# Conditioning weights loaded directly behind the block of the input projection that they follow, instead of a block on

## What is computed

```python
mod_x = (silu_c @ w_mod[i] + b_mod[i])[:, None, :]
mod_c = silu_cc @ w_mod[i] + b_mod[i]
sh_x, sc_x, g_x = jnp.split(mod_x, 3, axis=-1)
hx = rms_norm(x, norm_g[i]) * (1.0 + sc_x) + sh_x
...
px = hx @ w_in
q = apply_axial_rope(rms_norm(q, q_g), cos, sin)
...
x = x + g_x * yx
```

## Time and profile before

| | us |
|---|---|
| median of 3 runs | 2017.3 |
| lowest, highest | 2016.65, 2020.82 |
| the profiled execution | 2018.24 |
| its span (first to last instruction) | 2016.4 |
| mean granted TensorE clock | 0.985 |

### The profile page before, as it was taken

How to read it: one execution, slowest core, us unless ns; L and a number is a source line. 1 busy time by engine, 2 the same in 40 slices (tenths; PEclk the granted TensorE clock), 3 DMA queues, 4 the chain that set the end, 5 groups by cost and what they waited for, 6 DMA issues and landing times.

```text
span 2016.4 us, 28017 instructions
## 1 busy us (share of the span) xinstructions
PE 1916.3 (95%) x10575; PEld 1579.1 (78%) x10575; DVE 1455.0 (72%) x1546; ACT 1194.3 (59%) x1289; POOL 73.3 (4%) x66
## 2 busy tenths in 40 slices
PE   6999998998899899999889999999999999999997
PEld 4776677885687799998668888888888888888886
DVE  3655835227667665566588898989889898898985
ACT  3335815236456543444467777777777777777774
POOL 0110000003000000000010000000000000000000
PEclk9999999999999999999979999999999999999999
DMA  8451035436437355553469999999999999999993
GB/s 324 140 196 62 2 137 186 136 94 87 117 124 209 105 188 188 187 193 126 163 232 376 384 355 382 363 363 382 354 382 350 372 370 356 387 354 383 361 368 114
DMA packets 277031, 501.60 MB, mean 249 GB/s; under 512 B 26232, under 2 KB 53280, under 8 KB 276944
## 3 DMA queue, kind: packets, MB, share of 16 engines
q1 hardware_dynamic: 273648, 491.82, 69.8%
q0 software_dynamic: 2240, 8.03, 1.1%
q10 hardware_dynamic: 1056, 0.57, 0.1%
HBM read 498.25 MB, written 2.12 MB: 248 GB/s over the span
## 4 chain that ended last, share of the span: by engine, by line
PE 74%; issue 11%; DVE 7%; ACT 4%; DMA 2%; SPq 1%; POOL 1%; ACTq 0%; DVEq 0%; POOLq 0%
PE bank L1896 21%; PE bank L1897 21%; PE bank L1898 21%; SPq L667 1%; DVE w_lo L1154 1%; PE bank L2075 1%; ACT w_hi L767 1%; PE bank L2089 1%; PE bank L2365 1%; PE bank L2064 1%; DMA raw<-in_w_mod 1%; PE bank L1918 1%; PE bank L2127 1%; PE bank L2156 1%; PE bank L2399 1%
## 5 line engine op out<-in xcount | busy, mean ns | idle before, releaser
L1662 DVE TENSOR_TENSOR w_lo<-raw,w_hi 128x2048 fp32r<-128x2048 f32 x168 | 381.1, 2288 | 50.8 <-ACT w_hi L1057 50.8
L1662 DVE TENSOR_TENSOR w_lo_x<-raw_x,w_hi_x 128x2048 fp32r<-128x2048 f32 x168 | 382.8, 2290 | 42.0 <-ACT w_hi_x L1057 40.9
L1057 ACT ACTIVATE w_hi_x<-raw_x 128x2048 fp32r<-128x2048 f32 x168 | 323.2, 1924 | 128.7 <-PE bank L1898 126.7
L1154 DVE TENSOR_TENSOR w_lo<-raw,w_hi 128x2048 fp32r<-128x2048 f32 x98 | 224.1, 2290 | 217.7 <-ACT w_hi L767 217.6
L1057 ACT ACTIVATE w_hi<-raw 128x2048 fp32r<-128x2048 f32 x168 | 322.2, 1919 | 47.3 <-PE bank L1898 46.8
L767 ACT ACTIVATE w_hi<-raw 128x2048 fp32r<-128x2048 f32 x98 | 186.9, 1909 | 174.3 <-PE bank L1898 126.6
L1896 PE MATMUL bank<-h_hi,w_hi 128*128 128x256 f32 (+1 forms) x864 | 260.7, 302 | 4.6 <-DVE w_lo L1154 3.1
L1897 PE MATMUL bank<-h_lo,w_hi 128*128 128x256 f32 (+1 forms) x864 | 258.1, 299 | 0.0
L1898 PE MATMUL bank<-h_hi,w_lo 128*128 128x256 f32 (+1 forms) x864 | 258.0, 299 | 0.0
L1896 PE MATMUL bank<-w_hi,xe_hi 128*128 128x512 f32 x612 | 244.2, 399 | 0.0
L1898 PE MATMUL bank<-w_hi,xe_lo 128*128 128x512 f32 x612 | 239.7, 392 | 0.0
(11 more groups left out here) (322 smaller groups left out, 3097.1 us busy)
## 6 DMA issues: line engine op xcount, KB each, us to landing
raw<-in_e_w SPq DMA_DIRECT2D x168, 1024.0 KB, 7.0
raw_x<-in_e_w SPq DMA_DIRECT2D x168, 1024.0 KB, 7.6
raw<-in_w SPq DMA_DIRECT2D x33, 1024.0 KB, 5.1
raw<-in_w_qkv SPq DMA_DIRECT2D x24, 1024.0 KB, 5.2
raw<-in_w_mod SPq DMA_DIRECT2D x19, 1024.0 KB, 5.3
raw<-in_b_w_in SPq DMA_DIRECT2D x16, 1024.0 KB, 5.8
raw<-in_a_w_in SPq DMA_DIRECT2D x9, 1024.0 KB, 7.3
raw<-in_w_o SPq DMA_DIRECT2D x8, 1024.0 KB, 5.5
```

The costliest lines, as they stand in the source:

```text
L1057: nc.scalar.activation(ring6(w_hi, w_hi_x, n, 1)[:, 0, :], ring6(raw, raw_x, n, 1)[:, 0, :], ACT.Copy).then_inc(x_hi_ready, 1)
L1154: nc.vector.tensor_tensor(w_lo[:, split_slot(m), :], raw_unit(m), w_hi[:, split_slot(m), :].bitcast(F32), ALU.subtract).then_inc(lo_ready, 1)
L1662: nc.vector.tensor_tensor(ring6(w_lo, w_lo_x, n, 1)[:, 0, :], ring6(raw, raw_x, n, 1)[:, 0, :], ring6(w_hi, w_hi_x, n, 1)[:, 0, :].bitcast ...
```

## The change

```diff
@@ -116,8 +116,8 @@
             if (name, cb) == ("a_in", 0):
                 mod_columns(*mods_between[name, cb])
             one_unit(name, w, cb, 1)
-            if (name, cb - 1) in mods_after:
-                mod_columns(*mods_after[name, cb - 1])
+            if (name, cb) in mods_after:
+                mod_columns(*mods_after[name, cb])
 
     mod_columns(0, 0, 1)
     columns_and_mods("a_in", a_w_in)
```

## The result

| | before | after |
|---|---|---|
| median | 2017.43 us | 2075.42 us |
| lowest, highest of 4 | 2016.65, 2020.82 | 2072.35, 2076.07 |
| span of the profiled execution | 2016.4 | 2074.2 |
| mean granted TensorE clock | 0.985 | 0.973 |

Slower by 58.0 us, ratio 1.0278, 95% interval 1.0266 to 1.0289. (The ratio and its interval are estimated from all the runs; the quotient of the two medians is 1.0287.) I had said 2070, between 2054 and 2081.

What follows compares the result with a forecast made beforehand. TensorE, busy 95% of the span, was taken as the bound. 41 us at six edges plus 12 us of lower clock gave 53; 2017.3 + 53 = 2070 us, range 2054 to 2081.

Steps and rivals of the forecast that it cites:

- The slot rule and the load behind M(c)a: At six edges the next block's second-half load waits until M(c)a, the first conditioning unit, is used: 1.0 + 0.1 us.
- ACT's order as the second link: At the edges ACT rounds both halves of the next block before emptying the first bank; rounding 1.92 us, emptying 0.6.
- The edges: From a block's end to the next block's start, six in all: 28 us more in `a_in`, 13 in `b_in`.
- the terms of edge 1/2: Block 1 to 2 of `a_in`: conditioning, load, rounding, emptying, DVE, copy and turn; block 2 starts at 108.1, +16.9 us.
- The clock: Behind each of six new idle stretches the TensorE clock falls, costing 2.0 us each, 12 us together.
- Rival 1: The clock doesn't fall at the edges: 41 us alone, 2058 us; chance 0.12.
- Rival 2: At the edges only load, rounding and first bank count, PE's turns don't wait: 39 us, 2056 us; chance 0.07.
- Rival 3: At six edges loads take 7.5 instead of 5.2 us, or the clock costs 3.0 each: 2076 to 2084; chance 0.13.
- Rivals 4: Conditioning weights land a block early, PE's waits for them vanish: 8.4 us faster, 2009 us; chance 0.03.
- 5: The change does nothing measurable, losses and gains cancelling, with the six waits shrunk to 1 us each; chance 0.02.
- The signs: ACT waits six times, 10 us and more; PE idle 7, about 11, 10, 8 or more; block 4 starts near 186.
- What follows as a whole: Behind block 4 of `a_in` nothing is changed, so attention a and the rest move as a whole.

Runs made afterwards that it cites:

- run 9: Changed kernel with the conditioning pair a half block further ahead, between the halves of its own block, from block 1 on; 2109.22 us, ratio 1.0445.
- 1: Changed order of loads, with ACT emptying its banks before rounding the next block's second half, in all blocks; 2031.05 us, ratio 1.0060 against before.
- 10: Changed order of loads, with ACT emptying its banks first at the six changed edges alone; 2026.89 us, ratio 1.0038 against before.
- 11: Order of loads of before, with ACT emptying its banks first at the same six edges alone; 2031.85 us, ratio 1.0067 against before.
- run 2: Order of loads of before, with ACT emptying its banks before rounding the next block's second half, in all blocks; 2038.52 us, ratio 1.0090 against before.
- 4: Conditioning pair between the next block's two halves, and ACT emptying its banks first everywhere; 2021.16 us, ratio 1.0008 against before.
- run 12: Conditioning pair between the next block's halves and ACT emptying first, in blocks 0 to 3 of `a_in` alone, rest as before; 2016.48 us, ratio 0.9991.
- 7: Changed kernel plus 26 matmuls with unused result behind the conditioning matmuls at each of the two edges of `b_in`; median 2071.82 us.
- 8: The changed kernel measured again, on the chip and in the rounds of the run with added dense matmuls; median 2073.82 us.

## Why the prediction was right, point by point

- *The slot rule and the load behind M(c)a*: right. A2h1's load is issued 96.67 - 95.57 = 1.1 behind the block's end (1.0 + 0.1 predicted); run 9 moved the chain as the rule says.
- *ACT's order as the second link*: right; runs 1, 10 and 11 show it. I had named it from the code. What I had not seen is the third link in the other direction: DVE's own order, a low part between two tiles, so that a late rounding is never free (run 2). That didn't touch the forecast, but the expectation of 2; those of 1, 4 and 12 were missed as well, as told there.
- *The edges, predicted and measured* (the terms of edge 1/2 add up to 108.2 and not to 108.1, which changes nothing): 8.8 and 8.6; 15.0 and 15.2; 13.3 and 13.4; 12.8 and 13.6; 8.6 and 9.3; 8.6 and 9.6. The two of `b_in` were too low because of one term: from issue to rounding there pass 5.9 and 6.1 us instead of 5.2 (in `a_in` 5.0 and 5.1). At the edge 3/4, 0.8 too low, the turns run at the lower clock: 1.09 for four and 1.71 for the eight small matmuls, where I had 0.5 and 0.8 at the full one. From the turns' start to block 4 there pass 2.45 us instead of 1.3; what stands ahead of them took 11.2 instead of 11.5.
- *The clock*: 12 us predicted, 11.5 measured, 1.3 to 2.4 at an edge where I had put 2.0, shown by runs 7 and 8 at two of the six. The 11.5 are the blocks alone; the turns ahead of them run at the lower clock too, and the edges hold that. So the clock was priced a little too low, and the closeness of 12 and 11.5 is in part luck. Rival 1, that it would not fall, is out.
- *Rival 2*, handovers off the path: out. PE waits 11.13 us for `q_a` at edge 1/2. *Rival 3*, loads dearer: in part, by 0.7 and 0.9 us at the two edges of `b_in`; why there and not in `a_in` isn't shown. *Rivals 4 and 5* are out; PE's waits for the conditioning weights did vanish, 5.4 us in all, and six longer ones came.
- *The signs*: ACT waits for the half at all six edges, 14.1, 14.9, 20.5, 21.1, 13.2 and 11.3 us. PE's longest waits are 6.7, 11.1, 9.3 and 7.8 in `a_in`, where I had 7, about 11, 10 and 8 or more. Block 4 starts at 184.83 (186), block 2 of `b_in` at 405.32 (403).
- *What follows as a whole*: right. Attention a and all behind it are moved, and nothing there takes the loss up.
- The sum was 53, measured 58.0 (57.8 between the spans): the edges gave 44.1 instead of 41, the clock 11.0 instead of 12 (11.5 less the 0.5 of before), and 2.7 came in the rest, which I had put at nothing; 1.7 of them are the place at L2165.

## What to carry to other kernels

In a shared ring of buffers, list the load that reuses each slot, and ask *when* the slot's present owner is used: a transfer that is brought forward holds its slot until its use, and what is gated is the load one ring length behind it. Then look at the engine that handles that load and at what stands behind it in program order; here a rounding ahead of four full banks turned one late 1 MB load into a stop of PE. An order of loads and an order of work on the consuming engines are one decision: each of the two edits tried alone was slower, and the pair that fitted best came to no measurable difference.

## What the runs showed of the hardware that I had not expected

What the lower clock takes from the work behind an idle stretch didn't grow with the stretch: 1.3 us lost in the block behind 11.1 us of waiting (edge 1/2; the four turns ahead of it lose some 0.4 more, 0.74 us from their start to the block's instead of 0.38 in run 12), 2.4 behind 7.7 (edge 1/2 of `b_in`). Unrelated matmuls of full width in the stretch kept the granted clock at 1.00 throughout and gave back 4.8 us at two edges, the edges themselves as long within 0.1 us.

The same wait doesn't always have the same price. Ahead of L2165 PE waits 1.93 or 1.94 us in all fourteen traces; in nine the eight matmuls behind it take 5.40 us, in five 3.70. What decides it isn't shown here. It bounds what one trace can prove about a microsecond or two.
